# Gate product in seven products with sums in PSUM, and attention with one pair of scores at each key step

## The chip, the cores and the metric

The kernel runs on one core of one Trainium2 chip, as one program written instruction by instruction for the five engines: TensorE (matmul), VectorE, ScalarE, GpSimd and SyncE, which here only issues transfers. Engines meet at semaphores alone. The metric is the time of one execution on the device in microseconds, the median of three runs.

## The reference

Two blocks follow one another on 1024 tokens of width 1024, all in fp32. The first is a mixer with a state-space part and an attention part behind a common input projection, then a mixture of experts; the second has pooling, a second state-space model and a gated feed-forward. The change touches the first mixer:

```
proj = hx @ w_in                          # z, q, xbc, dt, k, v
y = (y_forward + y_backward + xs * skip) * silu(z)
y = y / rms(y over each half of the channels) * ssd_norm_g
q, k = rope(rms_norm(q)), rope(rms_norm(k))   # 16 query heads, 4 key heads, 64 wide
o = softmax(q k^T) v                      # 1024 queries, 1280 keys: 256 of context
out = concat(y, o) @ w_out
```

Here z is a product of hx (1024 x 1024) with a 1024 x 1024 piece of w_in.

## The kernel before

Every engine has one list of instructions, a function per stage, and works through it in order. The stages around the change are ssd (the scans), gate, qkv, att and out.

**Gate.** `ZUNITS` are 16 units, a column half n of z by a tile t of 128 tokens. TensorE (`pe_gate`) makes a unit of eight products (k = 0 to 7) with 512 columns into one of four PSUM banks. ScalarE (`act_gate`) applies Silu, VectorE (`dve_gate`) multiplies y by it, ScalarE squares and sums the row, VectorE scales the sum, ScalarE takes the root, and VectorE inverts it and scales y (the unit is normed). Silu and root need different tables, so each unit loads two. `turn(u - 2)` transposes the normed unit two units back in four TensorE instructions, and `turned_gate` on VectorE copies it with the gain into mixl. The weights lie in a ring of three slots of 2 MB (`slot(j)`, `load_panels`), and `panel_free` says after which product a slot may be filled again. Panel J_Z is there as the stage begins; J_Z + 1 is loaded by `sp_gate` once ssd has ended.

**qkv.** 18 jobs: ten of k and v (tiles of 128 tokens, the last two of context, whose hc was spilled to DRAM and is read back), eight of q. `pe_qkv_product(j)` is one 512-column product of eight steps for k and v. The products run one job ahead of the turns: turn of job 0 behind product 1. Before the turn VectorE norms and rotates the job (L1135 to L1166), and both engines begin the first job only when the gate stage has ended. In the gate stage product 0 stands between the last two turns:

```
turn(2 * LT - 2)
pe_qkv_product(eng, 0)
turn(2 * LT - 1)
```

**Attention.** 16 jobs (`NJOB`), each a pair of heads by 512 queries. For each of ten key tiles (kt, a step) `shifted(j, kt)` makes the transposed scores of both heads (L1273, 64 rows of the array each, head e on row half e) plus a shift per query (L1279, bf16), ScalarE takes the exponential (L1330) into prT, GpSimd adds the exponentials up (L1348) and TensorE multiplies them with v in `pv` (L1289, 128 rows and 64 columns of the array), in two batches of five after steps 4 and 9. Three banks hold the shifted scores; a head's bank is free again when its exponential is made. The shift is the row maximum, and for it the scores are made a second time in row form, one and two jobs ahead: `scores(j, pair)` with 12 pairs per job, a query tile by a piece of 512, 512 or 256 keys (L1254), whose maxima VectorE takes (`largest`, L1366). `BESIDE` says which pairs are made at which step: one each, and two at steps 2 and 7. Their results, the turned shifts (`turn_shifts`) and the row sums (`row_sums`, L1297) share three banks in turn; the use after next but one waits until a bank's result is read. `split` makes the shift of three bf16 parts (L1375 to L1380), `scale` takes the reciprocal of the row sums (L1393) and scales the output (L1395).

## Time and profile before

| what | us |
|---|---|
| median of 3 runs (3095.95 to 3100.65) | 3097.41 |
| span of the profiled execution, first to last instruction | 3093.3 |
| TensorE busy | 2916.4 (94%) |
| VectorE busy | 1591.3 (51%) |
| GpSimd busy | 1076.2 (35%) |
| ScalarE busy | 740.7 (24%) |
| gate stage, from 486.0 to | 604.6 |
| of it at a granted clock of 0.50 | 486.0 to 490.2 |
| qkv stage, to | 805 |
| attention, to about | 1330 |

The profiled execution's own time has no entry beside its span; the median of the timed runs is 4.1 us above the span. Times in the rows are us from the first instruction. In the rows PE is TensorE's matmul, PEld its weight load, DVE VectorE, ACT ScalarE and POOL GpSimd; L1254 is line 1254 of the kernel. An fp32 matmul of the program is two matmul instructions in the trace. The granted clock is TensorE's, 1.00 for 2.4 GHz and 0.50 for 1.2 GHz.

### The profile page before, as it was taken

The numbers are of one execution on the slowest core, as the hardware profiler recorded it, in microseconds if no ns is written. First come the engines' busy times: TensorE is split into PE (matmuls) and PEld (weight loads), VectorE is DVE, ScalarE is ACT, GpSimd is POOL, SyncE is SP. The second block draws the span as 40 slices with busy tenths as digits, with TensorE's granted clock in tenths as the row PEclk, the third lists the DMA queues.
The fourth block names the chain that finished last, engine by engine and source line by source line (L and its number), as shares of the span: only waits on it lengthen the run. The fifth ranks groups of instructions, "written<-read, shape, count | busy, mean of one in ns | idle before, by whom it ended". The sixth has DMA issues, their size and how long they took to land. (4 is left out here: it accounts for less than half of the span.)

```text
span 3093.3 us, 28722 instructions
## 1 busy us (share of the span) xinstructions
PE 2916.4 (94%) x10163; PEld 1457.1 (47%) x10163; DVE 1591.3 (51%) x2480; ACT 740.7 (24%) x1557; POOL 1076.2 (35%) x971
## 2 busy tenths in 40 slices
PE   7998999999899999999969994988999999999999
PEld 4554554444455555444544442566444444444443
DVE  2433884345666666555654434446543444444446
ACT  2223755411133333300211115222030000000002
POOL 0002871000176767710022002832023445555442
PEclk9998999999899999999969996999999999999999
DMA  7001332100100000020178987003020111111101
GB/s 276 21 0 41 90 96 72 54 28 1 55 1 1 1 1 1 1 66 11 68 259 320 358 352 239 22 0 123 0 82 27 41 41 49 66 49 41 41 14 61
DMA packets 130686, 237.51 MB, mean 77 GB/s; under 512 B 25544, under 2 KB 81520, under 8 KB 120688
## 3 DMA queue, kind: packets, MB, share of 16 engines
q1 hardware_dynamic: 120016, 206.11, 18.8%
q0 software_dynamic: 5760, 16.78, 1.8%
q10 hardware_dynamic: 4768, 12.79, 1.1%
q8 instruction: 81, 1.33, 0.2%
q14 instruction: 61, 0.50, 0.1%
HBM read 235.65 MB, written 26.22 MB: 85 GB/s over the span
## 5 line engine op out<-in xcount | busy, mean ns | idle before, releaser
L3597 DVE TENSOR_TENSOR arena_d<-arena_d,ps 128x512 f32<-128x512 f32 x154 | 101.8, 684 | 389.2 <-PE ps L3472 389.2
L1366 DVE TENSOR_REDUCE arena_b<-ps 128x1 f32<-128x512 f32 (+1 forms) x384 | 217.3, 599 | 146.5 <-PE ps L1254 146.0
L3437 POOL TENSOR_TENSOR arena_b<-arena_b,arena_d 128x512 f32<-128x512 f32 x120 | 150.8, 1271 | 362.7 <-DVE arena_d L3619 361.3
L1348 POOL TENSOR_TENSOR arena_b<-arena_b 128x512 f32<-128x512 f32 x182 | 224.6, 1268 | 94.5 <-ACT arena_b L1330 94.5
L1254 PE MATMUL ps<-arena_d,arena_a 64*128 64x512 f32 (+1 forms) x768 | 237.1, 541 | 3.6 <-DVE arena_b L1357 2.9
L1273 PE MATMUL ps<-arena_a,arena_d 64*128 64x512 f32 x640 | 220.0, 607 | 2.4 <-ACT arena_b L1330 1.8
L3616 DVE TENSOR_TENSOR arena_b<-arena_b,ps 128x512 f32<-128x512 f32 x240 | 159.0, 685 | 32.7 <-POOL arena_b L3437 23.7
L1077 PE MATMUL ps<-ring,arena_b 128*128 128x512 f32 x384 | 167.4, 592 | 0.0
L564 PE MATMUL ps<-arena_b,ring 128*128 128x512 f32 x384 | 167.1, 593 | 0.0
L1330 ACT ACTIVATE arena_b<-ps 128x512 f32<-128x512 f32 x214 | 116.1, 595 | 212.8 <-PE ps L1279 212.8
L3472 PE MATMUL ps<-arena_a,ring 128*128 128x512 f32 x352 | 156.0, 602 | 3.0 <-DMA ring<-in_w_up 3.0
L1254 PEld LDWEIGHTS ps<-arena_d,arena_a 64*128 64x128 f32 x768 | 114.0, 190 | 72.9 <-issue 41.9
L2110 PE MATMUL ps<-ring,arena_a 128*128 128x512 f32 (+1 forms) x352 | 143.3, 600 | 3.4 <-ACT arena_a L2158 3.4
L782 POOL TENSOR_TENSOR ring<-m_le,arena_t 128x512 f32<-128x512 f32 x32 | 40.7, 1271 | 284.6 <-ACT arena_d L654 280.9
L1348 POOL TENSOR_TENSOR arena_b<-arena_b,arena_t 128x512 f32<-128x512 f32 x96 | 118.8, 1269 | 46.1 <-ACT arena_t L1330 46.1
L1273 PEld LDWEIGHTS ps<-arena_a,arena_d 64*128 64x128 f32 x640 | 88.7, 185 | 79.3 <-issue 33.2
L3522 ACT ACTIVATE arena_d<-arena_d 128x512 f32<-128x512 f32 x44 | 27.7, 630 | 394.9 <-DVE arena_d L3597 394.9
L3488 PE MATMUL ps<-arena_c,arena_t 128*128 128x512 f32 x240 | 116.0, 592 | 0.0
L988 PE MATMUL ps<-ring,arena_b 128*128 128x512 f32 x256 | 114.4, 601 | 0.8 <-DVE arena_a L729 0.8
L1772 POOL MEMSET arena_t<- 128x64 f32 x4 | 0.4, 151 | 325.0 <-ACT arena_a L1121 325.0
L564 PEld LDWEIGHTS ps<-arena_b,ring 128*128 128x128 f32 x384 | 72.0, 190 | 86.0 <-issue 86.0
L1077 PEld LDWEIGHTS ps<-ring,arena_b 128*128 128x128 f32 x384 | 71.7, 190 | 84.2 <-issue 84.2
(614 smaller groups left out, 5492.3 us busy)
## 6 DMA issues: line engine op xcount, KB each, us to landing
ring<-in_w_gate SPq DMA_DIRECT2D x33, 1024.0 KB
ring<-in_w_up SPq DMA_DIRECT2D x33, 1024.0 KB
ring<-in_w_down SPq DMA_DIRECT2D x33, 1024.0 KB
ring<-in_w_in SPq DMA_DIRECT2D x10, 2048.0 KB, 9.8
ring<-in_w_mod SPq DMA_DIRECT2D x32, 512.0 KB, 3.8
yslots<-arena_a ACTq DMA_DIRECT2D x24, 512.0 KB, 4.5
arena_d<-in_w_gate SPq DMA_DIRECT2D x10, 1024.0 KB
arena_d<-in_w_up SPq DMA_DIRECT2D x10, 1024.0 KB
```

The lines of the kernel that those rows point to most:

```text
L564: mm = eng.matmul(ps[:, b, 0:n], w[:, k, (m % 4) * P:(m % 4 + 1) * P], src[:, k, :], start=(k == 0), stop=(k == KT - 1))
L1077: mm = eng.matmul(ps[:, 2 * (j % 2) + n, :], h_tile(k, t), w[:, k, :], start=(k == 0), stop=(k == KT - 1))
L1254: eng.matmul(ps[:, shared("s", u), 0:k1 - k0], qT[rows, pr, q0:q0 + P], kT[rows, pr // 2, k0:k1], start=True, stop=True).then_inc(s_S, 1)
L1273: eng.matmul(ps[:, 3 + (n + e) % 3, :], kT[rows, pr // 2, kt * P:(kt + 1) * P], qT[rows, pr, qs], start=True, stop=False)
L1330: eng.activation(prT[n % NPR], ps[:, 3 + n % 3, :], ACT.Exp).then_inc(s_ex, 1)
L1348: eng.tensor_tensor(acc, first, prT[n % NPR], ALU.add).then_inc(s_pa, 1)
L1366: eng.tensor_reduce(mx3[j % 2][:, t, e, piece:piece + 1], ps[:, shared("s", u), 0:k1 - k0], AX.X, ALU.max).then_inc(s_mx, 1)
L2110: mm = eng.matmul(ps[c0:c1, s % 2, :], xsT[s % 2][:, k, c0:c1], sguw[j % 3][:, :, k, :], start=(k == 0), stop=(k == KT - 1))
L3437: eng.tensor_tensor(o, o, dsum[0 if a == "a12" else 1], ALU.add).then_inc(s_comb, 1)
L3472: mm = eng.matmul(bank_of("gu", b, w, p), lhs, rhs, start=(k == 0), stop=(k == HK - 1))
L3488: eng.matmul(bank_of("dn", b, i, p), lhs[p], rhs[p], start=True, stop=True).then_inc(dn_done, 1)
L3616: ins = eng.tensor_tensor(o, o, src, ALU.add)
```

## The change

The gate product takes the tokens in two halves of four tiles, the reduction in two halves of four steps and the columns in two halves. For each of four groups g (tile g and tile g + 4) seven products of four steps make the four units c11, c12, c21 and c22. GpSimd makes the sums of the input tiles (`pool_z_sums`, four of 128x512 per group), VectorE four sums of the weight quarters (128x2048 each, once). p2 is accumulated onto p1, p3 onto p5 and p4 onto p7 in PSUM; ScalarE copies p1 before p2 is added. VectorE adds what is left (u2, u3, c22, c12, c21). The order of the products is `ZORDER`, that of the units a new `ZUNITS`, and the turns stand where `TURNS` says. The product of q/k/v job 0 goes behind p6 of the last group, that of job 1 ahead of the last two turns. The reload of hc, and the q panels behind it, wait for the whole gate product.

In attention each step has one pair of scores. The sixth pair of each half job comes between the second and the third of the five `pv` steps. The order of the shared banks follows, and VectorE takes that pair's maxima behind the copy of the shifts and ahead of `split` and `scale`.

```diff
+        KH = KT // 2
+        NG = LT // 2
+        ZORDER = [("p1", 0), ("p2", 0)]
+        for g in range(NG):
+            ZORDER += [("p5", g), ("p7", g), ("p6", g), ("p1", g + 1), ("p3", g), ("p2", g + 1), ("p4", g)]
+        ZORDER = [w for w in ZORDER if w[1] < NG]
+        NZP = len(ZORDER)
+        ZUNITS = [("c11", 0)] + [(c, g + (c == "c11")) for g in range(NG) for c in ("c22", "c12", "c11", "c21")
+                                 if c != "c11" or g + 1 < NG]
...
+        ZBANK = {"p1": (0, 0), "p2": (0, 0), "p5": (1, 1), "p3": (1, 1), "p7": (2, 3), "p4": (2, 3), "p6": (3, 2)}
...
+        panel_free[J_Z] = panel_free[J_Z + 1] = (s_z, NZP)
 
         def sp_gate(eng):
             after(eng, "ssd")
             load_panels(eng, J_Z + 1, J_KV)
...
+            load_panels(eng, J_KV, J_Q)
+            eng.wait_ge(s_z, NZP)
+            eng.dma_start(hc.rearrange("p k n -> p (k n)"), hc_dram).then_inc(s_spill, 16)
+            load_panels(eng, J_Q, NPAN1)
...
+        def pool_z_sums(eng):
+            after(eng, "ssd")
+            for g in range(NG):
+                z1, z2, z3, z4 = zsum[g % 2]
...
+                eng.tensor_tensor(z2, z1, hx_part(0, 0, g), ALU.subtract).then_inc(s_zi, 1)
+                eng.wait_ge(s_zi, ZI0 + 4 * g + 3)
+                eng.tensor_tensor(z4, hx_part(0, 1, g), z2, ALU.subtract).then_inc(s_zi, 1)
...
+            def product(name, g):
+                z1, z2, z3, z4 = zsum[g % 2]
+                left, right = {"p1": (hx_part(0, 0, g), z11), "p2": (hx_part(0, 1, g), z21),
+                               "p3": (z4, z22), "p4": (hx_part(1, 1, g), zt4), "p5": (z1, zt1),
+                               "p6": (z2, zt2), "p7": (z3, zt3)}[name]
...
+                elif name == "p2":
+                    eng.wait_ge(s_zc, ZC0 + g + 1)
+                elif name == "p3":
+                    eng.wait_ge(s_zi, ZI0 + 4 * g + 4)
+                    eng.wait_ge(s_za, zadded("c22", g))
...
+                for k in range(KH):
+                    mm = eng.matmul(zbank(name, g), left[:, k, :], right[:, k, :],
+                                    start=(k == 0 and name not in ("p2", "p3", "p4")),
+                                    stop=(k == KH - 1), skip_group_check=True)
                 mm.then_inc(s_z, 1)
-                if u >= 2:
-                    turn(u - 2)
+
+            TURNS = {("p6", 0): ("c11", 0)}
+            for g in range(NG - 1):
+                TURNS[("p2", g + 1)] = ("c22", g)
+                TURNS[("p5", g + 1)] = ("c12", g)
+                TURNS[("p7", g + 1)] = ("c11", g + 1)
+                TURNS[("p3", g + 1)] = ("c21", g)
+            TURNS[("p4", NG - 1)] = ("c22", NG - 1)
+            for name, g in ZORDER:
+                product(name, g)
+                if (name, g) == ("p6", NG - 1):
+                    pe_qkv_product(eng, 0)
+                if (name, g) in TURNS:
+                    turn(ZUNITS.index(TURNS[(name, g)]))
+            pe_qkv_product(eng, 1)
             turn(2 * LT - 2)
-            pe_qkv_product(eng, 0)
             turn(2 * LT - 1)
...
         def act_gate(eng):
             after(eng, "ssd")
-            for u, (n, t) in enumerate(ZUNITS):
-                eng.wait_ge(s_z, u + 1)
-                if u >= 4:
-                    eng.wait_ge(s_zg, u - 3)
-                eng.activation(zs[u % 4], ps[:, u % 4, :], ACT.Silu).then_inc(s_zs, 1)
+
+            def copied(g):
+                eng.wait_ge(s_z, zmade("p1", g))
+                if g >= 2:
+                    eng.wait_ge(s_za, zadded("c21", g - 2))
+                eng.copy(zu2[g % 2], zbank("p1", g)).then_inc(s_zc, 1)
+
+            copied(0)
+            for u, (c, g) in enumerate(ZUNITS):
+                t, n = ztile(c, g)
+                if c == "c11":
+                    eng.wait_ge(s_z, zmade("p2", g))
+                    if u >= 4:
+                        eng.wait_ge(s_zg, u - 3)
+                    eng.activation(zs[u % 4], zbank("p2", g), ACT.Silu).then_inc(s_zs, 1)
+                else:
+                    eng.wait_ge(s_za, zadded(c, g))
+                    eng.activation(zs[u % 4], zs[u % 4], ACT.Silu).then_inc(s_zs, 1)
+                if c == "c22" and g + 1 < NG:
+                    copied(g + 1)
...
+            def adds(u):
+                c, g = ZUNITS[u]
+                u2 = zu2[g % 2]
+                if c == "c22":
+                    eng.wait_ge(s_zc, ZC0 + g + 1)
+                    eng.wait_ge(s_z, zmade("p6", g))
+                    added("u2", g, u2, u2, "p6")
+                    eng.wait_ge(s_za, zadded("u2", g))
+                    added("u3", g, zu3, u2, "p7")
+                    eng.wait_ge(s_za, zadded("u3", g))
+                    added("c22", g, zs[u % 4], zu3, "p5")
...
+            wait_panel(eng, J_Z)
+            wait_panel(eng, J_Z + 1)
+            weight_sum(1, zt1, z12, z11)
+            weight_sum(2, zt3, z22, z12)
+            weight_sum(3, zt2, z22, zt1)
+            weight_sum(4, zt4, z21, zt2)
+            for u, (c, g) in enumerate(ZUNITS):
+                t, n = ztile(c, g)
+                adds(u)
+                if u >= 1:
+                    normed(u - 1)
                 v = y[:, t, n * HALF:(n + 1) * HALF]
...
+                if u >= 4:
+                    turned_gate(u - 4)
+                squared(u)
+            normed(2 * LT - 1)
+            for u in range(2 * LT - 4, 2 * LT):
                 turned_gate(u)
...
         def pe_qkv(eng):
             for j in range(1, NJ + 1):
-                if j < NJ:
+                if 1 < j < NJ:
                     pe_qkv_product(eng, j)
                 i = j - 1
                 kind, t = JOBS[i]
...
                 if i >= 2:
                     eng.wait_ge(s_qkTc, i - 1)
                 else:
-                    eng.wait_ge(s_zTc, 2 * LT - 2 + 2 * i)
+                    eng.wait_ge(s_zTc, 2 * LT)
...
-        BESIDE = (((1, 6),), ((1, 7),), ((1, 8), (1, 9)), ((1, 10),), ((1, 11),),
-                  ((2, 0),), ((2, 1),), ((2, 2), (2, 3)), ((2, 4),), ((2, 5),))
+        BESIDE = tuple((a, p) for a, p0 in ((1, 6), (2, 0)) for p in range(p0, p0 + 5))
 
         GROUP = 5
+        BETWEEN = {GROUP - 1: (1, 11), NT - 1: (2, 5)}
+        PV_FIRST = 2
...
                     shifted(j, kt)
-                    for ahead, pair in BESIDE[kt]:
-                        if j + ahead < NJOB:
-                            scores(j + ahead, pair)
+                    ahead, pair = BESIDE[kt]
+                    if j + ahead < NJOB:
+                        scores(j + ahead, pair)
                     if kt == NT - 1 and j + 1 < NJOB:
                         turn_shifts(j + 1)
                     if kt == NT - 1 and j >= 1:
                         row_sums(j - 1)
-                    if kt % GROUP == GROUP - 1:
-                        for i in range(kt + 1 - GROUP, kt + 1):
-                            pv(j, i)
+                    if kt in BETWEEN:
+                        for i in range(GROUP):
+                            if i == PV_FIRST:
+                                ahead, pair = BETWEEN[kt]
+                                if j + ahead < NJOB:
+                                    scores(j + ahead, pair)
+                            pv(j, kt + 1 - GROUP + i)
...
                 largest(1, pair)
             for j in range(NJOB):
                 for kt in range(NT):
-                    for ahead, pair in BESIDE[kt]:
+                    ahead, pair = BESIDE[kt]
+                    if j + ahead < NJOB:
+                        largest(j + ahead, pair)
+                    if kt == NT - 1 and j + 1 < NJOB:
+                        shifts(j + 1)
+                    if kt in BETWEEN:
+                        ahead, pair = BETWEEN[kt]
                         if j + ahead < NJOB:
                             largest(j + ahead, pair)
                     if kt == GROUP - 1 and j + 1 < NJOB:
                         split(j + 1)
-                    if kt == NT - 1 and j + 1 < NJOB:
-                        shifts(j + 1)
                     if kt == NT - 1 and j >= 1:
                         scale(j - 1)
```

## Rows read from the trace of the kernel before

**Rows 1.** Page, busy time of the engines (share of the span) and count

```profile
PE 2916.4 (94%) x10163; PEld 1457.1 (47%) x10163; DVE 1591.3 (51%) x2480; ACT 740.7 (24%) x1557; POOL 1076.2 (35%) x971
```

**Rows 2.** Busy time by stretch: PE, PEld, DVE, ACT, POOL, PE clock, DMA

```profile
480.00:604.50 124.50, 121.98 (x333) 58.08 (x332) 33.51 (x80) 63.64 (x93) 0.94 (x5) 0.97 0.19 62
...
835.00:1330.00 495.00, 492.59 (x2416) 245.47 (x2414) 310.74 (x485) 176.22 (x322) 353.09 (x288) 1.00 0.00 1
```

**Rows 3.** Groups by line and shape (count, busy, mean ns, idle before, releaser)

```profile
L1025 DVE TENSOR_TENSOR arena_a<-arena_a,arena_d 128x512 f32<-128x512 f32 x15 | 10.4, 692 | 58.5 <-ACT arena_d L1003 58.5
...
L1145 DVE TENSOR_TENSOR arena_t<-arena_t,rowc 128x1024 f32<-128x1024 f32 x8 | 9.8, 1224 | 0.3
```

**Rows 4.** Timeline, ScalarE and VectorE, of one gate unit (start, us, instruction)

```profile
502.12 0.60 ACT L1003 ACTIVATE arena_d<-ps 128x512 f32<-128x512 f32 x1 [0.62 <-PE ps L988]
...
505.73 1.28 ACT L1003 ACT_TABLE_LOAD   x1
...
506.01 0.49 DVE L1033 TENSOR_SCALAR arena_a<-arena_a,arena_d 128x512 f32<-128x512 f32 x1
```

**Rows 5.** DMA issued at 486.0 (count, KB, us from issue to landing)

```profile
ring<-in_w_in SPq DMA_DIRECT2D x1, 2048.0 KB, 8.9
```

**Rows 6.** Timeline, TensorE and VectorE, from gate to q/k/v

```profile
611.95 7.03 PE L1077 MATMUL ps<-ring,arena_b 128*128 128x512 f32 x16
618.82 0.60 PE L1093 MATMUL ps<-ident,arena_c 128*128 128x128 f32 x4
...
612.15 0.69 DVE L1016 TENSOR_TENSOR arena_c<-ps,cols 128x512 f32<-128x512 f32 x1 [2.61 <-PE ps L978]
...
617.09 0.43 DVE L1166 COPY arena_c<-arena_t 128x512 f32<-128x512 f32 x1
```

**Rows 7.** Busy time by stretch, around waits of TensorE (columns of rows 2)

```profile
1623.90:1627.20 3.30, 0.05 (x1) 0.02 (x1) 3.03 (x11) 1.50 (x4) 2.98 (x2) 0.95 0.32 132
1627.20:1630.20 3.00, 2.99 (x8) 1.10 (x10) 1.36 (x5) 0.00 (x0) 0.86 (x1) 0.50 0.41 85
...
808.00:817.90 9.90, 9.90 (x22) 5.20 (x22) 4.98 (x9) 0.00 (x0) 0.00 (x0) 0.50 0.02 2
```

**Rows 8.** Timeline, TensorE, one job of attention

```profile
1002.03 0.59 PE L1254 MATMUL ps<-arena_d,arena_a 64*128 64x256 f32 x2
1002.55 1.08 PE L1289 MATMUL ps<-arena_b,arena_d 128*64 128x512 f32 x4
...
1005.17 1.89 PE L1289 MATMUL ps<-arena_b,arena_d 128*64 128x512 f32 x8
1006.99 1.13 PE L1273 MATMUL ps<-arena_a,arena_d 64*128 64x512 f32 x4
...
1038.35 1.13 PE L1273 MATMUL ps<-arena_a,arena_d 64*128 64x512 f32 x4
```

**Rows 9.** Timeline, the step with two pairs, and the reciprocal

```profile
1012.03 1.80 PE L1254 MATMUL ps<-arena_d,arena_a 64*128 64x256 f32 x7
...
1013.14 0.18 PEld L1254 LDWEIGHTS ps<-arena_d,arena_a 64*128 64x128 f32 x1 [0.35 <-DVE arena_b L1366]
...
1013.47 0.59 PE L1273 MATMUL ps<-arena_a,arena_d 64*128 64x512 f32 x1
1013.68 0.59 PE L1254 MATMUL ps<-arena_d,arena_a 64*128 64x512 f32 x1
...
1019.09 3.36 DVE L1393 RECIPROCAL arena_b<-ps 128x512 f32<-128x512 f32 x1 [0.59 <-PE ps L1297]
```

**Rows 10.** Timeline, TensorE, last job, which has no scores beside it

```profile
1304.56 0.38 PE L1279 MATMUL ps<-arena_b 64*128 64x512 bf16 x2
...
1305.62 0.18 PEld L1273 LDWEIGHTS ps<-arena_a,arena_d 64*128 64x128 f32 x1 [0.66 <-ACT arena_b L1330]
```

**Rows 11.** Timeline, VectorE, first and last cast of the split

```profile
1034.69 1.22 DVE L1376 CAST arena_b<-arena_b 128x8 bf16<-128x8 f32 x1
...
1037.58 0.19 DVE L1380 CAST arena_b<-arena_b 128x8 bf16<-128x8 f32 x1
```

More of the change, by code:

```diff
@@ L947, in build @@
         mixl = view(arena_c, 0, KT, L)
+        qss = sb("qss", [P, 2, 2, HEADS])
         zs = [view(arena_d, i * HALF, HALF) for i in range(4)]
-        sqz = view(arena_d, 2 * DSSD, HALF)
-        ssum = view(arena_d, 3 * DSSD, 2 * LT)
-        rst = view(arena_d, 3 * DSSD + 16, 2 * LT)
+        sqz = view(arena_d, 4 * HALF, HALF)
+        zu2 = [view(arena_d, (5 + i) * HALF, HALF) for i in range(2)]
+        zu3 = view(arena_d, 7 * HALF, HALF)
+        ssum = qss[:, 0, 0, :]
+        rst = qss[:, 0, 1, :]
         s_rope = sem("rope_loaded")
@@ L955, in build, with zmade, zadded, zbank @@
         s_zT, s_zTc = sem("gate_transposed"), sem("gate_copied")
-        panel_free[J_Z], panel_free[J_Z + 1] = (s_z, LT), (s_z, 2 * LT)
-        ZUNITS = [(n, t) for n in range(2) for t in range(LT)]
+        s_zi, ZI0 = s_hd, 4 * (NT - 2)
+        s_zw, ZW0 = s_cbm, LT
+        s_zc, ZC0 = s_exp, NQUAD
+        s_za, ZA0 = s_hxv, 12
+        KH = KT // 2
[7 more added lines that the diff above has]
+                                 if c != "c11" or g + 1 < NG]
+        ZADDS = [(a, g) for g in range(NG) for a in ("u2", "u3", "c22", "c12", "c21")]
+        ZBANK = {"p1": (0, 0), "p2": (0, 0), "p5": (1, 1), "p3": (1, 1), "p7": (2, 3), "p4": (2, 3), "p6": (3, 2)}
+        z11, z21 = slot(J_Z)[:, 0:KH, :], slot(J_Z)[:, KH:, :]
+        z12, z22 = slot(J_Z + 1)[:, 0:KH, :], slot(J_Z + 1)[:, KH:, :]
+        zt1, zt2 = view(arena_d, 8 * HALF, KH, HALF), view(arena_d, 12 * HALF, KH, HALF)
+        zt3, zt4 = z12, view(arena_c, 16 * HALF, KH, HALF)
+        zsum = [[view(arena_t, (4 * i + j) * HALF, KH, P) for j in range(4)] for i in range(2)]
+        def zmade(name, g):
+            return ZORDER.index((name, g)) + 1
+        def zadded(name, g):
+            return ZA0 + ZADDS.index((name, g)) + 1
+        def zbank(name, g):
+            return ps[:, ZBANK[name][g % 2], :]
+        def ztile(c, g):
+            return g + NG * (c[1] == "2"), int(c[2] == "2")
+        def hx_part(i, k, g):
+            t = g + NG * i
+            return hx[:, k * KH:(k + 1) * KH, t * P:(t + 1) * P]
+        panel_free[J_Z] = panel_free[J_Z + 1] = (s_z, NZP)
         def sp_gate(eng):
@@ L1012, in dve_gate, with weight_sum, added, squared @@
         def dve_gate(eng):
+            after(eng, "ssd")
+            def weight_sum(i, dst, a, b):
+                eng.tensor_tensor(dst, a, b, ALU.subtract).then_inc(s_zw, 1)
+                if i < 4:
+                    eng.wait_ge(s_zw, ZW0 + i)
+            def added(name, g, dst, a, src):
+                eng.tensor_tensor(dst, a, zbank(src, g), ALU.add).then_inc(s_za, 1)
+            def adds(u):
[7 more added lines that the diff above has]
+                    added("u3", g, zu3, u2, "p7")
+                    eng.wait_ge(s_za, zadded("u3", g))
+                    added("c22", g, zs[u % 4], zu3, "p5")
+                elif c == "c12":
+                    eng.wait_ge(s_z, zmade("p3", g))
+                    added("c12", g, zs[u % 4], u2, "p3")
+                elif c == "c21":
+                    eng.wait_ge(s_z, zmade("p4", g))
+                    added("c21", g, zs[u % 4], u2, "p4")
+            def squared(u):
+                t, n = ztile(*ZUNITS[u])
+                eng.wait_ge(s_zss, 2 * u + 1)
+                eng.tensor_scalar(ssum[:, u:u + 1], ssum[:, u:u + 1], 1.0 / HALF, EPS_RMS,
+                                  ALU.mult, ALU.add).then_inc(s_zq, 1)
+            def normed(u):
+                t, n = ztile(*ZUNITS[u])
+                v, r = y[:, t, n * HALF:(n + 1) * HALF], rst[:, u:u + 1]
+                eng.wait_ge(s_zss, 2 * u + 2)
+                step(eng, eng.reciprocal(r, r), s_zq, 2 * u + 2)
+                eng.tensor_scalar(v, v, r, None, ALU.mult).then_inc(s_zn, 1)
             def turned_gate(u):
-                n, t = ZUNITS[u]
+                t, n = ztile(*ZUNITS[u])
                 eng.wait_ge(s_zT, u + 1)
@@ L1235, in build @@
                     takes("r", j - 1)
+                if kt in BETWEEN:
+                    ahead, pair = BETWEEN[kt]
+                    if j + ahead < NJOB:
+                        takes_pair(j + ahead, pair)
         takes("r", NJOB - 1)
@@ L1407, in dve_att @@
                 for kt in range(NT):
-                    for ahead, pair in BESIDE[kt]:
+                    ahead, pair = BESIDE[kt]
+                    if j + ahead < NJOB:
+                        largest(j + ahead, pair)
+                    if kt == NT - 1 and j + 1 < NJOB:
+                        shifts(j + 1)
+                    if kt in BETWEEN:
+                        ahead, pair = BETWEEN[kt]
                         if j + ahead < NJOB:
```

74 lines of the change are left out of this document (41 added, 33 removed).

## Prediction

> **What bounds the kernel now.** I read the page first: TensorE is busy for 94% of the span and every other engine for about half of it or less [rows 1]. So time is won or lost only where TensorE's own work or its waits change. The busy times by stage then say how full TensorE is where the change acts: 122.0 of 124.5 us in the gate product, 492.6 of 495 us in attention [rows 2]. In neither stage is there room behind TensorE, so every new wait shows. The groups of instructions of the gate stage give VectorE's idle time before its multiply: 58.5 us, and what ends it is ScalarE's activation, which itself waits for TensorE (0.62 us in the unit shown) [rows 3, 4]. Last I read the timelines at the four places where the new order meets something: a gate unit, the hand-over from gate to q/k/v, a job of attention, and the last job.
>
> An fp32 product is two matmul instructions in the trace. Sixteen take 6.87 us (611.95 to 618.82), so one takes 0.429 us at full clock [rows 6].
>
> **Gate product: what is saved.** 128 products of 512 columns become 7 x 4 x 4 = 112. That is 32 instructions fewer, 32 x 0.429 = **-13.7 us**. The 16 turns stay.
>
> **Gate product: new waits, in order of time** (the stage starts at 486.0, at half clock until 490.2).
> 1. p1 and p2 of the first group are neighbours, and p2 waits until ScalarE has copied p1. An activation of this size takes 0.60 us [rows 4], with about 0.15 us of signalling each way: **+0.9** (0.6 to 1.2). In later groups p3 lies between.
> 2. The second weight panel is now needed at once, not eight units later. It is issued as the stage starts and lands 8.9 us later [rows 5], at 494.9. The first weight sum (128x2048) follows: a 128x512 sum takes 0.69 us and a 128x1024 one 1.22 us, so 0.53 per 512 more, 2.3 us [rows 3]. p5 can start at 497.3. TensorE has done p1 (5.6 us, five instructions at half clock), the wait, and p2 (3.4) at 496.0: **+1.4** (0 to 1.6). The three other weight sums take 2.3 each against 3.43 for a product and stay hidden.
> 3. GpSimd makes its input sums of the second group at that moment. In attention, with GpSimd adding beside it, a 128x8 cast of VectorE took 1.22 us, the same form 0.19 a little later [rows 11]. One such block costs 1.0, so this costs 0 to 1.0: I take **+0.6**, the nearest row being one where it happened.
>
> The Trainium skill (SBUF — State Buffer, Who interferes with whom) says that a VectorE instruction with two SBUF inputs is blocked for the whole of a GpSimd instruction that reads SBUF and began first. By that rule a weight sum that meets a running GpSimd sum waits for its end, and the term would be the whole 1.0; without the rule it is nothing. The trace of before has the block in a small cast, and no VectorE sum of this size beside GpSimd in this stage.
> 4. The turn of the first unit stands right behind p6 of group 0. But VectorE norms unit 0 only after the three adds of unit 1, and the first of those needs p6. So TensorE waits for 3 x 0.69 + 0.49 [rows 3, 4], and for signals, gaps and a 128x1 reciprocal, some 0.6 together: **+3.2**.
> 5. After that I find no wait. A group is 7 x 3.43 + 4 x 0.44 = 25.8 us of TensorE. ScalarE's chain for a unit runs from its Silu at 502.12 to the end of the table load at 507.01, 4.9 us [rows 4], four units and a copy 20.2 us. VectorE's adds are 3.4 us per group. Each turn stands at least 3 us behind its norm, and the chain of c12, c11 and c21, which come close together, is caught up before the next c22.
> 6. The end. Before, the product of q/k/v job 1 (6.87 us) lies between the last gate turn and job 0's turn, and covers the last gain (VectorE, 612.15) and job 0's chain to 617.52 [rows 6]. Now that product comes ahead of the last two turns. From the end of the turn (611.95) to job 0's turn would then be 617.52 - 611.95 + 0.1 = **+5.7**, with nothing behind it.
> 7. The clock. After TensorE had idled 3.3 us in the slot stage the following 3.0 us ran at a granted clock of 0.50 (1.2 GHz), which costs 1.5; after the long idle between q/k/v and attention 9.9 us ran at 0.50, which costs 5 [rows 7]. For the wait of point 4: **+1.5** (0 to 3). For the 5.7 us: **+2.6** (0 to 5).
> Sum of the gate: -13.7 + 0.9 + 1.4 + 0.6 + 3.2 + 5.7 + 1.5 + 2.6 = **+2.2** (-2.8 with the low ends, +7 with the high ones). The spill's reload, and the q panels behind it, now start when the gate product ends; they are needed at jobs 8 and 10, 50 us and more later.
>
> **Attention: what is removed.** The two heads of a pair use the two row halves of the array and run side by side: a pair of 512-column instructions costs 0.429. A job is 31.36 us (1006.99 to 1038.35) [rows 8]. In the step with two score pairs the fourth score must wait for the reduction of the first one; its weight load waits until 1013.14 for VectorE. The first row half starts the next step at 1013.47, which is 0.14 later than 1012.03 + 0.43 + 0.86; the second starts its last score at 1013.68, is through at 1014.11, and so is 0.64 behind. Every step after it runs at full rate but keeps the lag, until the row halves meet at the p-by-v products [rows 9]. So a group of five steps loses 0.78 us, and this goes.
>
> **Attention: what is added, per group.**
> - The 256-column pair, before doubled up or last, now stands alone at the third step. From its constant term to the next step are 0.21 + 0.43 = 0.64 us. The second half of the next step needs the bank that ScalarE frees: in the last job, where no scores fill the time, that load starts 1.06 us after the constant term, and 0.10 more go into loading weights [rows 10]. So the second half falls behind by 1.17 - 0.64 = **+0.53**, kept to the end of the group like the lag before.
> - The sixth pair in the middle of the p-by-v products: the array goes from full rows to row halves and back. Into row halves, 1005.17 + 8 x 0.2145 = 1006.89 against 1006.99, and the first four instructions take 1.13, where four in steady order take 1.03: 0.21 with rounding. Out of them, 1002.55 against 1002.03 + 0.43, and 1.08 for the first four in place of 1.03: 0.14 [rows 8]. Together **+0.35**. The pair itself only moves.
> - In the second group the row sums now wait for the reduction of a 512-wide score instead of a 256-wide one: +0.05.
> That makes -0.78 + 0.53 + 0.35 = +0.10 in a first group, +0.15 in a second.
>
> **Attention: the reciprocal.** VectorE's 3.36 us reciprocal of the row sums starts at 1019.09, 12.1 us into the group that begins at 1006.99 (the second of a job), and is over at 1022.45, before the next group's first scores [rows 8, 9]. After the change VectorE reduces pair 5 first. That pair is scored behind the sums and two p-by-v steps: five steps 9.9, turn 0.4, row sums 0.9, p-by-v 1.7 and the change to row halves 0.1 make 13.0 after the group's start. Its two reductions of 0.4 us each are done at 14.5, the reciprocal at 17.9. And the order of the three shared banks changes: the row-sum bank is now three uses ahead of the next job's first score instead of its third, so that score waits for the reciprocal. The pair (0.54), the change back (0.14), three p-by-v steps (2.57) and the change to row halves (0.1) end at 16.4, the next step's own part takes 1.17, so its natural place is 17.57; it starts at 17.96 and reloads its weights (0.10): **+0.49** in the 13 jobs that have a scale and such a pair. Bounds 0 and 0.9.
> Sum: 15 x 0.10 + 14 x 0.15 + 13 x 0.49 = 1.5 + 2.1 + 6.4 = **+10.0**. The shift split after the sixth pair (3.1 us [rows 11]) ends before the next step's scores are there, so it is hidden.
>
> **Total.** +2.2 + 10.0 = +12.2. The profiled span is 3093.3; it becomes 3105.5. The median of the runs, 3097.41, lies 4.1 above the span, which I carry over: 3097.4 + 12.2 = **3109.6 us**. A change under 0.2% (6.2 us) can't be told from none in this kernel.
>
> **Rivals.**
> - *The second row half does not fall behind at the narrow step* (the other side). If the exponential frees its bank before the next step wants it, 29 groups lose 0.53 less, 15.4 us: 3094.2. For it: in a normal step the same wait costs only 0.09. Against: the interval of 1.06 us repeats in the last job. It decides when that interval falls under 0.64 + 0.10; if the clock also holds in the gate (-4.1), it is 3090, faster beyond the bound.
> - *The reciprocal stays hidden*: 6.4 less, 3103.2, within the bound. For it: only 0.4 us separate the two dates. Against: both dates are sums of steady intervals; job after job repeats within 0.02.
> - *Seven products win nothing*: if a unit's chain through both engines outlasts its place in every group (point 5 fails by 3 us, the smallest slack), TensorE waits four times for what it saved, +13.7: 3123. Against: 20.2 of 25.8 us.
>
> **How the numbers follow.** Forecast 0.52, its own range 3104 to 3117 (gate ends and the reciprocal's bounds in part). Row half does not lag 0.22, of which 0.12 under 3091.2 and 0.10 within. Reciprocal hidden 0.14, of which 0.12 within. No gain in the gate 0.12. The forecast's low end puts 0.04 within the bound. Faster 0.12, same 0.26, slower 0.62. The range 3092 to 3118 leaves about one in ten at each end.
>
> **What would show it.** Gate: 224 matmul instructions in place of 256; idle TensorE of about 3 us ahead of the first turn and about 6 us ahead of job 0's turn, each with a clock of 0.50 behind it. Attention: jobs of about 32.1 us in place of 31.36; in each group the load of the fourth step's second half waiting for ScalarE; the first score of a job waiting for VectorE's reciprocal. The prediction is wrong if jobs take 31.3 or less, or if TensorE has holes in every gate group.

## The result, and the profile after

The median over 10 runs is 3105.78 us (3099.65 to 3111.05). The kernel before, run beside it, has 3096.22 (3089.69 to 3100.65, 10 runs). The ratio is 1.0033 [1.0025, 1.0042], so the change makes the kernel slower by 9.6 us, beyond the 0.2% named in the prediction. The forecast was 12.2 us more; the median lies in the range, and in the forecast's own range of 3104 to 3117. The profiled execution after has a span of 3102.8 against 3093.3, 9.5 more.

The page's busy times of the kernel after:

```profile
PE 2911.2 (94%) x10131; PEld 1437.3 (46%) x10131; DVE 1581.6 (51%) x2504; ACT 743.0 (24%) x1561; POOL 1099.2 (35%) x987
```

TensorE has 32 instructions fewer than in [rows 1], as counted. It is busy for 5 us less and not for 13.7 less: in attention its busy time grew from 492.6 to 500.4 us, since it counts as busy while only one of its row halves works. The span still grew, so TensorE's waits grew too.

**The gate stage.** It now begins at 485.4. TensorE's timeline at its first group, with the wait in brackets:

```profile
491.82 3.70 PE L1071 MATMUL ps<-ring,arena_b 128*128 128x512 f32 x8 [0.75 <-ACT arena_d L1100]
497.86 3.67 PE L1071 MATMUL ps<-arena_d,arena_t 128*128 128x512 f32 x8 [2.33 <-DVE arena_d L1127]
501.37 3.60 PE L1071 MATMUL ps<-ring,arena_t 128*128 128x512 f32 x8
504.80 3.60 PE L1071 MATMUL ps<-arena_d,arena_t 128*128 128x512 f32 x8
511.29 0.66 PE L1033 MATMUL ps<-ident,arena_a 128*128 128x128 f32 x4 [2.89 <-DVE arena_a L1163]
```

and of VectorE and GpSimd in the same stretch:

```profile
494.51 3.20 DVE L1127 TENSOR_TENSOR arena_d<-ring 128x2048 f32<-128x2048 f32 x1 [7.71 <-DMA ring<-in_w_in]
497.75 2.29 DVE L1127 TENSOR_TENSOR ring<-ring 128x2048 f32<-128x2048 f32 x1
494.30 1.26 POOL L1022 TENSOR_TENSOR arena_t<-arena_b,arena_t 128x512 f32<-128x512 f32 x1
508.50 2.13 DVE L1132 TENSOR_TENSOR arena_d<-arena_d,ps 128x512 f32<-128x512 f32 x3 [2.27 <-PE ps L1071]
510.74 0.49 DVE L1163 TENSOR_SCALAR arena_a<-arena_a,qss 128x512 f32<-128x512 f32 x1
```

All three waits of the prediction are there: p2 behind ScalarE's copy, p5 behind the first weight sum, and the first turn behind three adds and a norm. The panel landed 9.0 us after it was issued (8.9 in [rows 5]). The first weight sum took 3.20 us where its three sisters took 2.29. GpSimd's sum had begun 0.21 us before it and ran for 1.26.

At the end of the gate TensorE's timeline answers to [rows 6]:

```profile
602.88 0.60 PE L1033 MATMUL ps<-ident,arena_a 128*128 128x128 f32 x4
603.32 7.03 PE L1235 MATMUL ps<-ring,arena_b 128*128 128x512 f32 x16
610.19 1.04 PE L1033 MATMUL ps<-ident,arena_a 128*128 128x128 f32 x8
616.85 1.11 PE L1251 MATMUL ps<-ident,arena_c 128*128 128x128 f32 x4 [5.63 <-DVE arena_c L1324]
617.76 9.39 PE L1235 MATMUL ps<-ring,arena_b 128*128 128x512 f32 x16
```

The product of job 1 is over, the last two turns are made, and TensorE then has nothing for 5.6 us. The product behind the wait takes 9.39 instead of 7.03. The turn in front of it takes 0.91 us (616.85 to 617.76), where it took 0.43 before (618.82 to 619.25). The busy times by stretch (columns of [rows 2]) say why, and show that the wait of the first turn did not have this effect here:

```profile
508.50:511.40 2.90, 0.11 (x1) 0.12 (x2) 2.69 (x6) 0.99 (x2) 0.00 (x0) 1.00 0.01 3
511.40:603.40 92.00, 92.00 (x257) 43.53 (x258) 39.82 (x82) 56.98 (x85) 11.24 (x8) 1.00 0.00 0
615.67:622.50 6.83, 5.65 (x10) 2.91 (x11) 4.58 (x16) 0.79 (x2) 0.00 (x0) 0.50 0.36 131
813.70:817.90 4.20, 3.85 (x14) 1.89 (x13) 3.49 (x7) 0.00 (x0) 0.00 (x0) 1.00 0.04 2
```

Behind the first turn's wait the clock stayed at 1.00, and TensorE was busy for every one of the next 92 us. Behind the 5.6 us it fell to 0.50 for 6.8 us. The last row is a stretch that ran at 0.50 before [rows 7]: the half-clock stretch ahead of attention ended at 813.6 instead of 817.9, and began later too (799.9 and 797.4).

**Attention.** One job, TensorE's timeline, answering to [rows 8]:

```profile
977.31 1.13 PE L1436 MATMUL ps<-arena_a,arena_d 64*128 64x512 f32 x4
...
983.64 0.38 PE L1442 MATMUL ps<-arena_b 64*128 64x512 bf16 x1
...
984.16 0.38 PE L1442 MATMUL ps<-arena_b 64*128 64x512 bf16 x1
...
990.41 0.70 PE L1417 MATMUL ps<-arena_d,arena_a 64*128 64x256 f32 x4
991.04 2.79 PE L1452 MATMUL ps<-arena_b,arena_d 128*64 128x512 f32 x12
993.77 1.13 PE L1436 MATMUL ps<-arena_a,arena_d 64*128 64x512 f32 x4
994.73 0.38 PE L1442 MATMUL ps<-arena_b 64*128 64x512 bf16 x2
995.22 1.13 PE L1417 MATMUL ps<-arena_d,arena_a 64*128 64x512 f32 x4
...
1009.32 1.13 PE L1436 MATMUL ps<-arena_a,arena_d 64*128 64x512 f32 x4
```

A job takes 1009.32 - 977.31 = 32.01 us in place of 31.36: its second group 16.46 (was 16.27), its first 15.55 (was 15.08). At the step behind the narrow pair the two heads' constant terms start 983.64 and 984.16: one row half is 0.52 behind, forecast 0.53. The first score of the next group waits for the reciprocal; VectorE's timeline and the weight load that waits:

```profile
991.14 0.76 DVE L1533 TENSOR_REDUCE arena_b<-ps 128x1 f32<-128x256 f32 x2 [2.68 <-PE ps L1417]
991.82 3.35 DVE L1560 RECIPROCAL arena_b<-ps 128x512 f32<-128x512 f32 x1
995.22 0.30 PEld L1417 LDWEIGHTS ps<-arena_d,arena_a 64*128 64x128 f32 x4 [0.81 <-DVE arena_b L1560]
```

The reciprocal starts 991.82 - 977.31 = 14.51 into the group; forecast was 14.5, and 12.1 it was before [rows 9].

**Where the 9.5 us of span are.** The gate's first product starts 0.6 earlier. From it to the last q/k/v product are 308.27 us (306.82 before), +1.45. From there to attention's first product are 1.6 less; the half clock just shown lies in this stretch. Attention is 504.5 us long in place of 495.6, +8.9. The stages behind add 1.3; their code is unchanged. -0.6 + 1.45 - 1.6 + 8.9 + 1.3 = 9.5.

### The profile page after: what moved, and what is told of

Same layout as the page of the kernel before. It is cut to its first block and busy times, and to the rows that moved or that the text cites. A ratio compares the mean times of both kernels' runs of the same rounds, so it can differ in the third digit from the quotient of the medians.

```text
span 3102.8 us, 28710 instructions
## 1 busy us (share of the span) xinstructions
PE 2911.2 (94%) x10131; PEld 1437.3 (46%) x10131; DVE 1581.6 (51%) x2504; ACT 743.0 (24%) x1561; POOL 1099.2 (35%) x987
## 5 line engine op out<-in xcount | busy, mean ns | idle before, releaser
L1417 PE MATMUL ps<-arena_d,arena_a 64*128 64x512 f32 (+1 forms) x768 | 218.6, 539 | 5.1 <-DVE arena_b L1524 2.9
L1436 PE MATMUL ps<-arena_a,arena_d 64*128 64x512 f32 x640 | 211.9, 611 | 2.5 <-ACT arena_b L1497 1.8
L1235 PE MATMUL ps<-ring,arena_b 128*128 128x512 f32 x384 | 169.8, 599 | 0.0
L1417 PEld LDWEIGHTS ps<-arena_d,arena_a 64*128 64x128 f32 x768 | 102.5, 188 | 88.4 <-issue 55.8
L1686 PE MATMUL ps<-ring,arena_c 128*128 128x512 f32 x256 | 110.3, 592 | 0.0
L3643 PEld LDWEIGHTS ps<-arena_a,ring 128*128 128x128 f32 x352 | 67.9, 193 | 89.2 <-issue 89.2
```

Of the source, the lines that this page charges most:

```text
L1235: mm = eng.matmul(ps[:, 2 * (j % 2) + n, :], h_tile(k, t), w[:, k, :], start=(k == 0), stop=(k == KT - 1))
L1417: eng.matmul(ps[:, shared("s", u), 0:k1 - k0], qT[rows, pr, q0:q0 + P], kT[rows, pr // 2, k0:k1], start=True, stop=True).then_inc(s_S, 1)
L1436: eng.matmul(ps[:, 3 + (n + e) % 3, :], kT[rows, pr // 2, kt * P:(kt + 1) * P], qT[rows, pr, qs], start=True, stop=False)
L3643: mm = eng.matmul(bank_of("gu", b, w, p), lhs, rhs, start=(k == 0), stop=(k == HK - 1))
```

## The experiments

The executions of one kernel differ by a few us, and the longer ones mostly have the lower mean clock. The traces differ as much in stages whose code is the same: the first gate product starts between 481.9 and 487.9, and the stages behind attention take 1760 to 1766 us. So each experiment is read twice: by the ratio to the kernel before on the same chip, and by lengths in the trace, above all that of a job, which repeats within 0.02 us.

**Each half of the change alone.** gate_only has the new gate stage and the attention of before; att_only the reverse.

```
 gate_only:   gate of after,  BESIDE ... dve_att of before
 att_only:    gate of before, BESIDE ... dve_att of after
```

> The seven products of the gate with the attention of before. My theory: the gate gains 13.7 us of products and loses it again to the copy of p1 (0.8), the wait for the weight sum (2.5), the turn of unit 0 (3.0), the uncovered chain of q/k/v job 0 (5.8) and half clock behind that (2.4), so the span is 0 to 2 us above that of before, and jobs of attention take 31.36 us. Rival, the gate is the whole loss: 8 to 10 us above before. Rival, the gate is a gain that attention hides: 5 to 13 us below before.

> The gate of before with the new order of attention. My theory: the first five-step group of a job takes 15.55 us (15.08 before), the second 16.46 (16.27), together 8.9 us over the stage; the span is 8 to 9.5 us above that of before. Rival, that attention is slow only because it now starts from another clock or another state of the banks after the gate: jobs of 31.36 us and a span within 2 us of before.

gate_only: 3098.32, ratio 1.0009 [1.0000, 1.0019]; jobs of 31.36 us. att_only: 3100.56, ratio 1.0022 [1.0012, 1.0031]; jobs of 32.01, attention 504.5 long. The two differences, +3.8 and +6.0, make 9.8 where the whole change made 9.6. So neither half wins anything, and nothing shows that they act on one another. How the loss is shared is less sure: the lengths in the traces give the gate 1.5 to 1.9 and attention 8.9. The medians gave the gate more and attention less than expected (0 to 2, and 8 to 9.5), but their intervals, 0 to 5.9 and 3.7 to 9.6 us, hold both readings. In gate_only the clock fell behind the first turn's wait, which it did not in the profiled execution of the kernel after; the stretch of its trace:

```profile
507.30:510.80 3.50, 3.48 (x8) 1.95 (x9) 0.69 (x1) 0.04 (x1) 0.00 (x0) 0.51 0.00 0
```

**The reciprocal ahead of the sixth pair's maxima.**

```diff
+                    if kt == NT - 1 and j >= 1:
+                        scale(j - 1)
                     if kt in BETWEEN:
                         ...
-                    if kt == NT - 1 and j >= 1:
-                        scale(j - 1)
```

> As the changed kernel, but VectorE makes scale(j - 1) with its 3.36 us reciprocal ahead of the maxima of the pair between the p-by-v steps. My theory: the first score of a job no longer waits for the reciprocal, the group that holds it goes from 15.55 to 15.18 us in 13 jobs, 4.8 us less in all; the pair's own maxima come at 16.2 to 17.0 us and are still in time. Rival, the 0.37 us is the price of the new bank order whatever VectorE does: no change. Rival, the late maxima hold up the second score of the next job instead: a gain of 2 us or less, or a loss.

3102.30, ratio 1.0023 [1.0013, 1.0033]. VectorE and the first weight load of the next score in its trace:

```profile
989.66 3.36 DVE L1560 RECIPROCAL arena_b<-ps 128x512 f32<-128x512 f32 x1 [0.34 <-PE ps L1460]
993.66 0.74 DVE L1533 TENSOR_REDUCE arena_b<-ps 128x1 f32<-128x256 f32 x2
995.59 0.41 PEld L1417 LDWEIGHTS ps<-arena_d,arena_a 64*128 64x128 f32 x4 [0.33 <-issue]
```

The load no longer waits for VectorE. First groups take 15.18 in place of 15.55, so the wait cost 0.37 each; attention is 499.6 long, 4.9 less, and 13 x 0.37 = 4.8. Second groups keep their 16.46. The wait is the reciprocal's, and nothing else hung on it. The median is 7.8 above that of the kernel before, in place of 9.6; a gain of 4.8 lies within the intervals.

**The narrow pair last.** The pair of 256 columns, at the third step of a group, trades places so that the 512-wide ones come first and both narrow ones stand at the fifth step and between the p-by-v products.

```diff
+        TILE_OF = [divmod(p0 + p, 3) for p0 in (0, 6) for p in (0, 1, 3, 4, 2, 5)]
...
-                t, piece = pair // 3, pair % 3
+                t, piece = TILE_OF[pair]
```

> As the changed kernel, but with the 256-key pair of each half job at the fifth step instead of the third, so that no step follows it before the p-by-v products. My theory: the second row half no longer falls 0.53 us behind in any of 29 groups, a job takes 30.95 us instead of 32.01, and the kernel is 15 us faster than the changed one and about 6 faster than before. Rival, the lag comes from the first p-by-v switch or from the row halves themselves: no change of the job. Rival, the lag appears at the end of the group instead: 0 to 3 us faster.

3092.76, ratio 1.0000 [0.9990, 1.0009]. Groups take 15.12 and 16.19, attention 494.2, 10.4 less than after. The median is 1.8 below that of the kernel before, where about 6 were expected. The expected 30.95 for a job was wrong: it is 31.32, since I had left out that the reciprocal's 0.37 stays. In the one early group without a reciprocal it is 14.75, 0.43 less than the 15.18 of after: the lag of 0.53 is gone but for the 0.09 of a normal step. In the second group another wait comes up, in TensorE's timeline:

```profile
1009.49 1.08 PE L1462 MATMUL ps<-arena_b,ones 128*64 128x512 f32 x4 [0.18 <-DVE arena_b L1535]
```

The row sums wait 0.18 for the maxima of the narrow score just ahead of them, so a second group gains 0.27 only.

**Both.** both_att is recip_first and narrow_last together, with the new gate.

> As the changed kernel, with the 256-key pair at the fifth step and the reciprocal ahead of the between pair's maxima. My theory: the two losses are apart from one another and add up: groups of 14.75 and 16.19 us, a job of 30.95, 5 us less than with the pair moved alone and 14 us less than the changed kernel; 4 to 6 us faster than before. Rival, with shorter groups the late maxima of the pair become the next wait: a job of 31.2 or more.

3092.15, ratio 0.9989 [0.9978, 1.0000]. Groups take 14.75 and 16.19, a job 30.95, 0.41 less than before the change, and attention 489.3. TensorE's timeline at the start of a group:

```profile
998.16 1.13 PE L1438 MATMUL ps<-arena_a,arena_d 64*128 64x512 f32 x4
...
999.34 1.02 PE L1419 MATMUL ps<-arena_d,arena_a 64*128 64x512 f32 x4
```

The two costs add up without a rest: 32.01 - 0.37 - 0.43 - 0.27 = 30.94. The median is 2.6 below that of the kernel before, where 4 to 6 were expected; its interval reaches from 0 to 6.8, so it can't tell the two apart.

**The narrow pairs doubled up instead of one between the p-by-v products.** On the order of narrow_last, both narrow pairs stand at the fifth step.

```diff
-        BESIDE = tuple((a, p) for a, p0 in ((1, 6), (2, 0)) for p in range(p0, p0 + 5))
-        BETWEEN = {GROUP - 1: (1, 11), NT - 1: (2, 5)}
+        BESIDE = tuple(((a, p),) if p < p0 + 4 else ((a, p), (a, p + 1)) for a, p0 in ((1, 6), (2, 0)) for p in range(p0, p0 + 5))
```

> No pair between the p-by-v steps: both 256-key pairs of a half job stand at its fifth step, the rest as with the narrow pair last. My theory: four changes between full rows and row halves per job go (0.35 us per group), but the second pair waits for the maxima of the one two uses before it, about 1.2 us for the pair in place of 0.78; the bank of the row sums is again waited for late, so the reciprocal is hidden. First groups 15.1 to 15.3 us, 31.2 to 31.7 per job. Rival, the changes between rows and halves cost more than the waits: under 14.75 in a first group.

3097.04, ratio 1.0003 [0.9993, 1.0013]; groups 15.09 and 16.27, a job 31.36, to 0.01 us that of the kernel before. So to have one pair at each step is worth 15.09 - 14.75 = 0.34 in a first group and 0.08 in a second, though each pair between p-by-v products pays two changes between full rows and row halves. In attention the idea of the change is sound; it is the place of the narrow pair and of the maxima that took more than it gave.

**Norm of unit 0 ahead of unit 1's adds.**

```diff
+                if u == 1:
+                    normed(0)
                 adds(u)
-                if u >= 1:
+                if u >= 2:
                     normed(u - 1)
```

> As the changed kernel, but VectorE norms unit 0 of the gate before it makes the adds of unit 1. My theory: TensorE's wait ahead of the first turn, 3.0 us, goes, and nothing takes its place; the gate stage is 3 us shorter by the trace. Rival, the root of unit 0 is late too (its multiply waits for the weight sums): 1 us or less is won. The whole kernel moves by less than can be told well, so the trace decides.

3104.10, ratio 1.0023 [1.0013, 1.0033]. The timeline of TensorE, VectorE and GpSimd:

```profile
507.62 3.60 PE L1071 MATMUL ps<-arena_d,arena_t 128*128 128x512 f32 x8
511.05 0.60 PE L1033 MATMUL ps<-ident,arena_a 128*128 128x128 f32 x4
498.86 3.24 DVE L1127 TENSOR_TENSOR ring<-ring 128x2048 f32<-128x2048 f32 x1
496.65 3.31 POOL L1022 TENSOR_TENSOR arena_t<-arena_b,arena_t 128x512 f32<-128x512 f32 x1
```

The first turn stands right behind p6 and waits for nothing: the 3.05 us are the order on VectorE, as step 4 had it. From the first gate product to the last q/k/v product are 305.65, 2.6 less than after, where 3 were expected. The median is 9.4 above that of the kernel before, in place of 9.6, less of a change than the runs scatter. In this trace p1 ran at full clock throughout, so p5 waited longer for the same panel (3.05) and then ran at half clock. This time it was the second weight sum that took 3.24, and GpSimd's sum that began beside the first one, at 496.65, took 3.31 in place of 1.26. This is the usual case: of the eight traces with the new gate and GpSimd's sums where they were, six have the long sum second, where no product waits for it, and two (after and narrow_double) have it first.

**GpSimd's second group of sums later.**

```diff
+                if g == 1:
+                    eng.wait_ge(s_zw, ZW0 + 4)
```

> As the changed kernel, but GpSimd holds its input sums of group 1 back until VectorE's four weight sums are made. My theory: the first weight sum takes 2.3 us as the three behind it, not 3.2, and TensorE's wait ahead of p5 of group 0 falls from 2.5 to 1.6 us; the sums of group 1 are needed 20 us later. Rival, the first sum is long for another reason (the panel's last bytes): 3.2 us again. The whole kernel moves by less than can be told, so the trace decides.

3107.12 (5 runs), ratio 1.0034 [1.0021, 1.0047]. Its VectorE timeline has all weight sums alike, and TensorE waits 1.49 us for the first one in place of 2.33:

```profile
497.08 2.29 DVE L1129 TENSOR_TENSOR arena_d<-ring 128x2048 f32<-128x2048 f32 x1 [7.78 <-DMA ring<-in_w_in]
499.40 2.29 DVE L1129 TENSOR_TENSOR ring<-ring 128x2048 f32<-128x2048 f32 x1
499.51 3.67 PE L1073 MATMUL ps<-arena_d,arena_t 128*128 128x512 f32 x8 [1.49 <-DVE arena_d L1129]
```

So the 0.9 us are GpSimd's, in the executions in which its sum begins just ahead of the first weight sum, and the 1.5 that are left are the panel's. The median, 12.1 above that of the kernel before in place of 9.6, didn't follow a difference so small; the intervals overlap.

**A product behind the last turns.**

```diff
-                if (name, g) == ("p6", NG - 1):
-                    pe_qkv_product(eng, 0)
...
-            pe_qkv_product(eng, 1)
+            pe_qkv_product(eng, 0)
             turn(2 * LT - 2)
             turn(2 * LT - 1)
+            pe_qkv_product(eng, 1)
```

> As the changed kernel, but the product of q/k/v job 0 comes behind the gate products and job 1's behind the last two turns, so that it covers the chain of job 0. My theory: the 5.8 us without work ahead of job 0's turn shrinks to under 1, the last turn waits at most 2 us for its norm, and the stretch at half clock goes with it (2.4 us): q/k/v begins its second product 5 to 8 us earlier. Rival, the last unit's norm is late by as much as was covered: no gain, the wait only moves ahead of the last turn.

3104.72 (6 runs), ratio 1.0033 [1.0020, 1.0046]. The idle 5.6 us and the half clock behind them are gone, but a wait has taken their place, in TensorE's timeline:

```profile
592.94 5.37 PE L1071 MATMUL ps<-ring,arena_t 128*128 128x512 f32 x8 [2.38 <-DVE arena_d L1131]
...
602.46 7.03 PE L1234 MATMUL ps<-ring,arena_b 128*128 128x512 f32 x16
609.33 1.04 PE L1033 MATMUL ps<-ident,arena_a 128*128 128x128 f32 x8
610.20 2.31 PE L1234 MATMUL ps<-ring,arena_b 128*128 128x512 f32 x5
```

Product 0 had stood between p6 and the last p3 and covered VectorE's three adds, which the p3 needs. Without it p3 waits 2.4 us and runs at half clock (5.37 for 3.60). By the trace, first gate product to last q/k/v product, there are 308.27 - 304.38 = 3.9 us less. Two differences at the stage's start, which are not the edit's, nearly cancel in this: 1.3 less ahead of the first turn, because GpSimd met the second weight sum, and 1.7 more behind it, because the clock fell. The product behind job 0's turn starts 1.5 us earlier, counted from the first gate product, not 5 to 8 as expected: the wait moved, as the rival had it, though to a place that neither had named. The median is 10.0 above that of the kernel before, so it shows no gain.

**The old gate with the mended attention.** old_gate_both_att has the gate stage of before and both_att's attention.

> The gate of before, with the new attention mended twice (256-key pair at the fifth step, reciprocal ahead of the between pair's maxima). My theory: jobs of 30.95 us, attention 6.3 us shorter than before, the kernel 5 to 7 us faster than before, 0.2%. Rival, the gain of the mended attention hangs on the new gate: the span within 2 us of before.

3084.96 (6 runs), ratio 0.9969 [0.9957, 0.9981]: 10.0 us faster than before, where 5 to 7 were expected and attention is 6.3 shorter; the rest is not explained. Its jobs take 30.95, as in both_att. With the new gate the same attention was 2.6 faster than before, so the new gate costs 7.5 us there, more than the 3.8 of gate_only. The traces of the two lie 2.9 apart from the first gate product to the last q/k/v product (307.61 and 304.74). Even the old gate differs by 2.1 in this length (306.82 before, 304.74 here, where its first products ran at full clock). So the price of the new gate is 1.5 to 7.5 us, and the runs say it no closer.

**All mends.** all_edits has both_att, norm0_first, pool_later and end_covered, and a last group in the order p7, p6, p5, p3, p4, so that one add alone stands between p5 and p3.

```diff
+        ZORDER[-5:] = [(p, NG - 1) for p in ("p7", "p6", "p5", "p3", "p4")]
...
+            del TURNS[("p5", NG - 1)]
+            TURNS[("p7", NG - 1)], TURNS[("p6", NG - 1)] = ("c12", NG - 2), ("c11", NG - 1)
...
+                    eng.wait_ge(s_z, zmade("p5", g))
```

> The changed kernel with attention mended twice and the gate mended four times: GpSimd's sums of group 1 later; unit 0 normed ahead of the adds of unit 1; the product of q/k/v job 1 behind the last turns; and p5 of the last group behind its p6, so that only one add stands between it and p3. My theory: attention 6.3 us shorter than before as above, and from the first gate product to the last of q/k/v 297 to 300 us (306.8 before, 308.2 in the changed kernel): the kernel 13 to 16 us faster than before. Rival, what is mended in the gate comes back as a wait before the last turn or at the last p3: 303 or more from the first gate product to the last of q/k/v, and 10 us faster or less.

3080.14 (5 runs), ratio 0.9948 [0.9934, 0.9961]: 14.9 us faster than the kernel before. What is left of the waits, from TensorE's timeline, and the end of the gate:

```profile
497.76 3.67 PE L1074 MATMUL ps<-arena_d,arena_t 128*128 128x512 f32 x8 [1.12 <-DVE arena_d L1131]
509.10 0.66 PE L1036 MATMUL ps<-ident,arena_a 128*128 128x128 f32 x4 [0.81 <-DVE arena_a L1168]
587.64 3.67 PE L1074 MATMUL ps<-ring,arena_t 128*128 128x512 f32 x8 [0.94 <-DVE arena_d L1136]
595.40:604.00 8.60, 8.60 (x29) 4.31 (x27) 5.49 (x12) 4.79 (x8) 0.00 (x0) 1.00 0.90 330
```

From the first gate product to the last q/k/v product are 297.81 us, 9.0 less than before, and no stretch behind 490.8 up to there is at half clock. So seven products do win, once their waits are covered. The copy costs 0.9, and the three waits above cost 1.3, 1.0 and 1.1, counted from the start of one instruction to the next (the idle time in brackets leaves out 0.16 of each). 13.7 - 0.9 - 3.4 = 9.4, where 9.0 were measured; p1 lost 0.2 more to the half clock than the old gate's first products did, and 0.2 are not assigned. Against old_gate_both_att, which has the same attention, the median is 4.8 lower, and this length 6.9 shorter.

## Why the prediction was right, and where its sizes were off

The direction and its two causes hold: new waits at both ends of the gate stage, and the narrow step and the reciprocal in attention. The size came out smaller, 9.6 in place of 12.2. Term by term:

**Gate.** 32 instructions fewer: shown. Point 1, the copy: TensorE's last instruction of p1 starts at 490.48 and p2 at 491.82, 1.34 later in place of 0.43, which is 0.9 as forecast. Points 2 and 3: p5 starts 2.5 us behind p2's end, against 1.4 + 0.6. The panel's part was right (pool_later leaves 1.5 to 1.6); GpSimd's was 0.9, where I had taken 0.6 between 0 and 1.0, and that it came at all is luck of timing: it shows in two of eight traces. The Trainium skill (SBUF — State Buffer, Who interferes with whom) has a VectorE instruction with two SBUF inputs blocked for the whole of a GpSimd instruction that reads SBUF and began first. The trace agrees within 0.14 us: GpSimd's sum ended at 495.56, and 2.29 from there is 497.85, against 497.71 measured. Point 4, the first turn: 3.05 against 3.2, and norm0_first shows the cause. Point 5, no waits after that: 92 us without a gap. Point 6: 5.8 from the end of the turn to job 0's turn, against 5.7. Point 7: the 5.6 us were followed by a half clock that cost 2.4 in the product and 0.5 in the turn ahead of it, 2.9 (taken: 2.6). Behind the first turn's wait the clock stayed full in this trace, so the 1.5 are nothing there. That is luck too: eight traces have this wait of 2.89 us, and in six of them, gate_only among them, the clock fell behind it and cost 1.4 to 1.7. -13.7 + 0.9 + 2.5 + 3.05 + 5.8 + 2.9 = +1.45, as measured. The low end of the gate, -2.8, was added up wrong: with 0.6, 0, 0, 3.2, 5.7, 0 and 0 it is -4.2. The measured value lies inside either.

**Attention.** First groups: +0.10, as forecast (15.18 against 15.08), and narrow_last shows that the narrow step takes 0.43 of the 15.18, where 0.53 less a normal step's 0.09 is 0.44. The 0.78 gained and the 0.35 for the changes of the array were not tested one by one; their difference holds, since both_att has 14.75 - 15.08 = -0.33 and -0.78 + 0.35 + 0.09 is -0.34. Second groups: +0.19, forecast 0.15. The reciprocal: it starts when it was said to, and costs **0.37 instead of 0.49**. This is the term that was most off, 13 x 0.12 = 1.6 us. In both_att, where nothing is in its way, that score starts 1.18 us into its group (998.16 to 999.34); here it starts at 1.45 (993.77 to 995.22). That is a wait of 0.27 where the working had 0.39: the score's natural place was 0.07 later (16.46 + 1.18 = 17.64 for 17.57) and its start behind the reciprocal 0.05 earlier (17.91 for 17.96). The 0.10 for loading the weights again did come: the next step starts 0.96 behind the score, in both_att 0.86. Sum 1.5 + 2.7 + 4.8 = 9.0, measured 8.9, forecast 10.0.

**What the sum didn't have.** The time from the last q/k/v product to attention is 1.6 less, with a half-clock stretch in it that is 6.8 us shorter than before, and stages whose code is unchanged take 0.7 more (-0.6 + 1.3). The first goes with where the clock fell in this execution, as far as the trace tells. What made the 0.7 no run shows; it is less than these stages differ from trace to trace. With the gate 0.75 and attention 1.1 below their forecasts, these make the 2.7 us between 12.2 and the 9.5 of the span.

**The rivals.** That the second row half doesn't fall behind: refuted, 0.52 us in the trace. That the reciprocal stays hidden: refuted by recip_first. That seven products win nothing: refuted in its mechanism, since no group after the first one waits; the stage did give its gain away, but at its two ends.

## What to carry to other kernels

- When a product is taken out of a full engine, list what the removed time had covered at both ends of the stage: here 13.7 us were saved in the middle, and three waits at the start and one at the end, with the half clock behind it, took 15.1 back.
- On an engine that works in order, a 3.4 us instruction with slack is safe only while nothing is put ahead of it; put the instruction that frees the bank needed next first.
- Where two operations share a loop in halves (here row halves with a bank each), a short companion step costs as much as a doubled one; give the short step the place where the halves meet anyway.

## What the runs showed of the hardware

- Sums of VectorE and GpSimd with both inputs in SBUF did not overlap: VectorE's of 128x2048 took 3.20 (3.24 in norm0_first) instead of 2.29 when a GpSimd sum of 128x512 was ahead of it, and GpSimd's took 3.31 instead of 1.26 when VectorE's had begun first.
- The same wait of TensorE is not always followed by a half clock. After 2.9 us ahead of the first turn the clock stayed at 1.00 in the kernel after and in recip_first, and fell in the six other traces with that wait, to 0.51 for 3.5 us in gate_only. After the 5.6 us it was 0.50 for 6.8 us, and it fell in all eight traces with that wait.
- Two row halves of the array keep a lag between them step after step (0.52 us here) until instructions over all rows follow, and a pair of 512-column instructions on the two halves costs as much as one over all rows (0.43 us each).
